# The expert down projection in three rounded passes, with its weights split in earlier stages

## The reference

```python
def grouped_moe(x, w_router, router_bias, w_gate, w_up, w_down):
    ...                                  # each row picks 2 of 16 experts, with weights comb
    for e in range(N_EXPERTS):
        h = jax.nn.silu(xt @ w_gate[e]) * (xt @ w_up[e])          # 1024 -> 256
        out = out + comb[:, e:e + 1] * (h @ w_down[e])            # 256 -> 1024

def hybrid_layer(x, ...):
    proj = x @ w_in                                               # 1024 -> 1536
    ...                                  # spatial gating and a state-space scan make the mix
    x = layer_norm(ALPHA * x + mix @ w_out, ln1_g, ln1_b)
    x = layer_norm(ALPHA * x + grouped_moe(x, ...), ln2_g, ln2_b)
```

## Time and profile before

| | us |
|---|---|
| median of 3 runs | 1359.34 |
| their range | 1359.04 to 1362.73 |
| the profiled execution: its own time | 1360.82 |
| the profiled execution: span of the instructions | 1359.2 |

### The profile page before, as it was taken

How to read it: one execution, slowest core, us unless ns; L and a number is a source line. 1 busy time by engine, 2 the same in 40 slices (tenths; PEclk the granted TensorE clock), 3 DMA queues, 4 the chain that set the end, 5 groups by cost and what they waited for, 6 DMA issues and landing times. The chain is left out here.

```text
span 1359.2 us, 22656 instructions
## 1 busy us (share of the span) xinstructions
PE 1198.9 (88%) x6653; PEld 957.0 (70%) x6654; DVE 893.2 (66%) x1975; ACT 462.5 (34%) x696; POOL 486.3 (36%) x557
## 2 busy tenths in 40 slices
PE   7999999799979768999999269999999999999910
PEld 6997999778767534888888257767767767767600
DVE  3452866468877573466667667777777777777586
ACT  4121010110012451222221225556556555556433
POOL 3008850210110033322322233545545545445267
PEclk9999899899979998999999579999999999999965
DMA  8555352564155322433332546787877777644484
GB/s 257 172 199 156 105 166 63 145 231 183 63 154 157 104 96 67 152 112 112 120 119 98 223 164 192 216 244 225 253 203 227 211 210 217 144 98 98 112 318 171
DMA packets 112875, 222.84 MB, mean 164 GB/s; under 512 B 51305, under 2 KB 68281, under 8 KB 103569
## 3 DMA queue, kind: packets, MB, share of 16 engines
q1 hardware_dynamic: 96368, 164.86, 36.3%
q0 software_dynamic: 15408, 55.12, 17.5%
q10 hardware_dynamic: 1040, 2.10, 0.4%
HBM read 144.34 MB, written 77.58 MB: 163 GB/s over the span
## 5 line engine op out<-in xcount | busy, mean ns | idle before, releaser
L2057 DVE TENSOR_TENSOR wgu<-w_raw,wgu (+1 forms) x192 | 226.0, 1219 | 52.5 <-ACT wgu L2144 52.5
L2244 PE MATMUL p_gu<-wgu,xg_high 128*128 x768 | 254.5, 413 | 4.5 <-DVE xg_low L2050 4.5
L2144 ACT CAST wgu<-w_raw (+1 forms) x192 | 187.1, 1050 | 19.4 <-SPq L1865 16.7
L2244 PEld LDWEIGHTS p_gu<-wgu,xg_high 128*128 128x128 f32 x768 | 145.2, 191 | 59.1 <-issue 31.3
L2267 PE MATMUL p_d<-wd,ht 128*128 x384 | 174.9, 598 | 1.8 <-DVE ht L2071 1.0
L2244 PE MATMUL p_gu<-wgu,xg_low 128*128 x384 | 152.0, 396 | 0.0
L2267 PEld LDWEIGHTS p_d<-wd,ht 128*128 128x128 f32 x384 | 69.0, 189 | 71.5 <-issue 71.2
L1730 PE MATMUL p_out<-w_out_high,mixt_high 128*128 128x512 f32 (+1 forms) x272 | 108.6, 399 | 10.5 <-POOL mixt_low L1507 10.5
L1730 PE MATMUL p_out<-w_out_high,mixt_low 128*128 128x512 f32 (+1 forms) x272 | 106.9, 393 | 0.0
L1730 PE MATMUL p_out<-w_out_low,mixt_high 128*128 128x512 f32 (+1 forms) x272 | 106.8, 393 | 0.0
L1936 POOL TENSOR_TENSOR spare_e<-nothing 128x1 f32<-128x1 f32 x48 | 9.3, 194 | 232.2 <-DVE yo L2077 232.2
(11 more groups left out here) (434 smaller groups left out, 2689.0 us busy)
## 6 DMA issues: line engine op xcount, KB each, us to landing
w_raw<-in_w_gate SPq DMA_DIRECT2D x16, 1024.0 KB, 4.8
w_raw<-in_w_up SPq DMA_DIRECT2D x16, 1024.0 KB, 7.7
wd<-in_w_down SPq DMA_DIRECT2D x16, 1024.0 KB, 4.7
acc_rows<-ax SPq DMA_DIRECT2D x18, 512.0 KB, 5.7
xin<-in_x_prompt SPq DMA_DIRECT2D x16, 512.0 KB, 6.3
sq<-sq_mats SPq DMA_DIRECT2D x16, 512.0 KB
z<-in_x_prompt SPq DMA_DIRECT2D x16, 512.0 KB, 4.2
x_rows<-x SPq DMA_DIRECT2D x16, 512.0 KB, 4.9
```

The costliest lines, as they stand in the source:

```text
L2057: low = tt(wgu[:, slot, 1, at], raw[:, slot, at], wgu[:, slot, 0, at].bitcast(F32), ALU.subtract)
L2144: nc.scalar.copy(wgu[:, slot, 0, at], raw[:, slot, at]).then_inc(hi_set, 1)
L2244: mm = t.matmul(pg[b][:, :, :], x[:, b, k, :], w[h][:, k], start=(k == 0 and x is xh and h == 0), stop=(k == KD - 1 and x is xl))
```

## The change

`down` is made in three rounded passes, twelve matmuls a tile. Both operands need two parts:

- `ht` becomes `ht_high` and `ht_low`. ACT makes the high part from PSUM (`hidden_high`), after three of its four weight quarters and ahead of the fourth and of `sl`. DVE's `tail` is now the subtraction, and waits for it.
- `w_down` is split before stage E, in 64 units of 128 x 512 (a quarter of an expert), and both parts go to HBM (`wd_dram`). Stage E loads 2 MB an expert where it loaded 1 MB. A unit is one load of 256 KB, a copy on ACT, a subtraction and two stores of 256 KB. 32 units are made in stage A, 8 in B (with POOL's subtraction), 24 in D, in places that are free at the time: six slots in A (two in `xin`, so that x rows have two buffers in place of four; four in parts of `ya` that are not yet written, where a row of 2 KB lies in four pieces of 512 bytes), three in B, and in D two parts of `ya` and `yb` a tile that `out` is done with (pieces of 512 bytes again). A table computed at the head of stage A gives one to two units for each step from n = 4 to 22; 21 of the 32 units are in pieces of 512 bytes.
- `ln2_g` and `ln2_b` are loaded after the last turning in place of at the head of stage E. SP's loop in D, and ACT's in B, are unrolled.

```diff
+            def units_at(n):
+                return [(j, s, sum(u[1] == s for u in UNITS[:j])) for j, (m, s) in enumerate(UNITS) if m == n]
...
+                def units(n):                                # stage A, SP
+                    for j, s, m in units_at(n - 2):
+                        sp.wait_ge(wd_low, j + 1)
+                        for h in range(2):
+                            sp.dma_start(wd_dram[h][j // 4, ...], wd_part(s, 1 - h, True).bitcast(F32)).then_inc(wd_st[s], 16)
+                    for j, s, m in units_at(n):
+                        if m:
+                            sp.wait_ge(wd_st[s], m * 32)
+                        elif s[0] == "x":
+                            sp.wait_ge(turned[int(s[1])], 1)
+                        sp.dma_start(wd_part(s, 0, False), wd_src[j // 4, :, j % 4]...).then_inc(wd_ld[s], 16)
...
                 def u_tile(i, f):                            # stage A, ACT
                     act.wait_ge(u_prod, i * FT + f + 1)
                     nc.scalar.activation(ya[:, f, i * XH:(i + 1) * XH], pu[f % 2][:, 0:XH],
                                          ACT.Gelu_apprx_tanh).then_inc(u_out, 1)
+                    for j, s, m in units_at(i * FT + f - 1):
+                        act.wait_ge(wd_ld[s], m * 16 + 16)
+                        nc.scalar.copy(wd_part(s, 1, True), wd_part(s, 0, False)).then_inc(wd_high, 1)
...
                     v.tensor_copy(ust[...], pxs[...]).then_inc(xs_out, 1)        # xs_tile, stage A, DVE
+                    for j, s, m in units_at(i * FT + f - 1):
+                        dve.wait_ge(wd_high, j + 1)
+                        v.tensor_tensor(wd_part(s, 0, True), wd_part(s, 0, False), wd_part(s, 1, True).bitcast(F32),
+                                        ALU.subtract).then_inc(wd_low, 1)
...
+                def units_in(i, b):                          # stage D, SP
+                    p = i * 2 + b
+                    sp.wait_ge(mix_low, p * 2 + 2)
+                    if p >= 5:
+                        sp.wait_ge(wd_st[b], (p - 3) // 2 * 64)
+                    for at, (e, q) in zip(areas(p), quarters(i, b)):
+                        sp.dma_start(ya[:, :, at], wd_src[bass.ds(e, 1), :, q]...).then_inc(wd_ld[b], 16)
+                def units_out(i, b):
+                    p = i * 2 + b
+                    sp.wait_ge(wd_low, p * 2 - 4)
+                    for at, (e, q) in zip(areas(p), quarters(i, b)):
+                        for h in range(2):
+                            sp.dma_start(wd_dram[h][...], (yb_r, ya_r)[h][:, :, at].bitcast(F32)).then_inc(wd_st[b], 16)
...
+                for i in range(2, CH // 2 - 1):
                     for b in range(2):
                         rows_in(i * 2 + b, b)
                         stores(i * 2 + b, b)
+                        units_out(i - 1 + b, 1 - b)
+                        units_in(i, b)
...
+                def units(i, b):                             # stage D, ACT
+                    act.wait_ge(wd_ld[b], i * 32 - 32 * (1 - b))
+                    for at in areas(i * 2 + b):
+                        nc.scalar.copy(yb_r[:, :, at], ya[:, :, at]).then_inc(wd_high, 1)
...
                         high(i * 2 + 2 + b, b)
                         tile(i * 2 + b, b, i)
                         score(i * 2 + b - 1)
+                        units(i, b)
...
+                def units(i, b):                             # stage D, DVE, after turn
+                    p = i * 2 + b
+                    dve.wait_ge(wd_high, p * 2 - 4)
+                    for at in areas(p):
+                        v.tensor_tensor(ya_r[:, :, at], ya[:, :, at], yb_r[:, :, at].bitcast(F32), ALU.subtract).then_inc(wd_low, 1)
...
                 def tail(i, b, first):                       # stage E, DVE
-                    dve.wait_ge(h_turned, i + 1)
-                    v.tensor_copy(ht[:, b], pt_h[:, :, :]).then_inc(ht_set, 1)
+                    dve.wait_ge(ht_high, i + 1)
+                    tt(ht[1][:, b], pt_h[:, :, :], ht[0][:, b].bitcast(F32), ALU.subtract).then_inc(ht_set, 1)
...
+                def hidden_high(i, b, first):                # stage E, ACT
+                    act.wait_ge(h_turned, i + 1)
+                    if not first:
+                        act.wait_ge(d_prod, i)
+                    nc.scalar.copy(ht[0][:, b], pt_h[:, :, :]).then_inc(ht_high, 1)
...
+                            for x, h in PARTS:               # stage E, PE, down
+                                mm = t.matmul(pd[m][:, :], ht[x][:, b, k, :], w[h][:, k, m * SUP:(m + 1) * SUP],
+                                              start=(k == 0 and x + h == 0), stop=(k == 1 and x == 1))
```

More of the change, by code:

```diff
@@ L266, in _ @@
                             sp.dma_start(sq_dram[pair, :, 0, :], s_mat[:, pair % 2, :]).then_inc(s_stored[pair % 2], 16)
+                        units(n)
+                        if i and f % 2 and 2 * i + 4 + f // 2 < CH:
+                            rows_in(2 * i + 4 + f // 2)
+                for s in SLOTS:
+                    sp.wait_ge(wd_st[s], sum(u[1] == s for u in UNITS) * 32)
                 sp.wait_ge(kz, 1)
@@ L396, in _ @@
                 act.wait_ge(w_v_in, 16)
+                for s in ("x2", "x3"):
+                    act.wait_ge(wd_st[s], sum(u[1] == s for u in UNITS) * 32)
                 for k in range(KD):
@@ L821, in _ @@
                 sp.wait_ge(vs_stored, 16)
+                for s in range(3):
+                    sp.wait_ge(wd_st[s], (3, 3, 2)[s] * 32)
                 sp.wait_ge(toep_in, L * 16)
@@ L1595, in _ @@
                 score(0, NS)
-                with act.Fori(1, CH // 2 - 1) as i:
+                for b in range(2):
+                    high(4 + b, b)
+                    tile(2 + b, b, 1)
+                    score(1 + b)
+                units(1, 1)
+                with act.Fori(2, CH // 2 - 1) as i:
                     for b in range(2):
@@ L1806, in hybrid_step @@
             hh = sb("hh", [P, 2, FF], where=pt)
-            ht = sb("ht", [P, 2, 2, P], where=pt)
+            ht = [sb(f"ht_{n}", [P, 2, 2, P], F32R, where=pt) for n in ("high", "low")]
+            assert pt.at <= base + 32 * KB
             pt = Place(nc, base + 35 * KB)
@@ L1874, in _ @@
                     down(e)
-                for dst, name in ((g2_row, "ln2_g"), (b2_row, "ln2_b")):
-                    sp.dma_start(dst[:], bass.AP(tensor=a[name].tensor, offset=0, ap=[[0, P], [1, D]])).then_inc(row2_in, 16)
                 for e in range(2):
@@ L1895, in _ @@
                 sp.wait_ge(prep_done, NT)
+                sp.wait_ge(x_turned, NT)
+                for dst, name in ((g2_row, "ln2_g"), (b2_row, "ln2_b")):
+                    sp.dma_start(dst[:], bass.AP(tensor=a[name].tensor, offset=0, ap=[[0, P], [1, D]])).then_inc(row2_in, 16)
                 sp.wait_ge(te_set, 3)
@@ L2139, in turn_b, with high @@
                         nc.scalar.copy(xh[:, b, h * 4:h * 4 + 4, :], pt_x[h]).then_inc(xt_hi, 1)
-                def high(slot):
-                    for c in range(4):
+                def high(slot, cs=range(4)):
+                    for c in cs:
                         at = slice(c * QG, (c + 1) * QG)
@@ L2164, in step @@
                         prep(i, not begun and b == 0, slot, ready)
+                    if begun or b:
+                        hidden_high(i - 1, 1 - b, not begun or begun == 1 and b == 0)
+                    if not last:
+                        high(slot, range(3, 4))
                     act.wait_ge(gu_prod, i + 1)
```

150 lines of the change are left out of this document (120 added, 30 removed).

## The result

The changed kernel took 1467.94 us (median of 4 runs, 1467.1 to 1468.96), the kernel before 1359.19 beside it: a ratio of 1.079 with a 95% interval of 1.078 to 1.081. The forecast of 1411 had the sign right and less than half of the size, and the range (to 1450) did not hold the time.

The account below looks back on a forecast made before the run. It took PE to bound the kernel, no stage having idle PE to hide delays. E -24, D +45, A +30, the rest +1 gave +52 on the profiled 1360.8, 1412.8, so a median of 1411, range 1365 to 1450.

Parts of the forecast that it names:

- Stage E: Expert stage: shorter `down` saves 0.5 us a tile, period 9.55, 47 periods -24 us; bounds -34 to -12.
- the 1.5 us behind it for slack: Expert tile: `xg_low` ends 1.5 us before the next `gate_up` wants it; the longer operand paths spend this.
- The late low part: Expert tile: ACT's copy then DVE's subtraction make `down` start about 0.15 us late.
- The pass: `down` in E: a rounded pass costs 0.228 us, so 12 take 2.74 for 3.46, 0.72 less.
- Rival 1: Stage E: DMA engines can't be filled past about 0.9, 10.2 us a tile, gain gone, total 1435; chance 0.16.
- the sign that I had named for it: Stage E: tiles 10 us or more apart would show the DMA-bound rival.
- Stage D: Stage D: transfers in SP's one queue form a lap of 18.4 us against 13.61 a tile, +45 us.
- the slack: Stage D: x1 is at first 4.8 us early, subtracted once from 11 laps x 4.8, about 48.
- My upper bound of +60: Stage D: with z's latency a lap of 19.5 us, +60; a lower PE clock stands inside it.
- Stage B: Stage B: eight units, with two x buffers fewer in A, cost 0 to +1 us behind PE work.
- Stage A: Stage A: units cost +11 to step 15, 16 from step 16, 3 for last stores: +30 us; bounds +10 to +45.
- The rival on the other side: Stages A and D: splitting hidden, deciding point a D lap under about 14 us, total 1336 to 1343; chance 0.10.

Follow-up runs that it names:

- x6: Changed kernel with D's loads one lap early, A's unit loads ahead of its stores, `gate_up` waiting for the fourth weight quarter only before its second half: 1382.83 us.
- x11: Changed kernel with D's loads early, ACT's fourth quarter back in place, only 21 units in A, none in B, E loading unsplit weights: 1368.94 us, E loop 481.1.
- x3: Changed kernel with `down`'s eight high-part matmuls first, the four low-part ones last behind the subtraction: 1462.96 us, E loop 484.3.
- x10: As x7, but A's units split one step later, one unit in steps divisible by four, none loaded in step 12: 1343.3 us, 0.989 of the kernel before.
- x7: Changed kernel with x3, x4 and x6's edits, 1 KB rows in A, B's subtraction on DVE, ACT's fourth quarter back in place: 1356.22 us, 0.997 of the kernel before.
- x4: Changed kernel with stage D's unit loads issued one lap ahead of ACT's copies: 1411.85 us, D 249.1.
- x5: As x4, plus 1 KB rows in A, B's POOL subtraction after `v_norm`, high-part matmuls first and split weight wait in E: 1378.05 us, E loop 463.0.

## Why the prediction was wrong

**Stage E is the step that failed.** The prediction wrote "I take 0.5 less a tile, a period of 9.55; 47 periods make -24". The traces gave 9.84 for a plain tile (from `down` to `down`, 1151.63 - 1141.79) and 10.97 for the next (1162.60 - 1151.63), which has a new expert's `gate_up` in it, as 15 of the 46 have; in the mean 10.28 against 10.16 before. Two costs were wrong, by size, and one was nearly right:

- *The fourth quarter's subtraction*, priced nowhere. I followed ACT's copy to `xg_low`, took the 1.5 us behind it for slack and stopped there. The earlier trace rows end with `xg_low`, but DVE's last instruction of a tile is that subtraction, in the kernel before too, where it left 0.39 us and not 1.5. A new expert's first product waits for it: 16 times, 0.82 us in the tile shown. The split wait (x6) brings 16 us, ACT's order alone (x11) 10.
- *The late low part*. I had 0.15; it is 0.17 to 0.24, and `down`'s first weights are then not loaded behind `p_xt`, 0.1 more. x3 removes both.
- *The pass*: 0.23 for 0.228. `down` in x3 takes 2.84 where I had 2.74, so PE gives back 0.62 of the 0.72.

Without the first two, E gains more than was hoped: 486.4 to 456.5 in x10, 30 us. Rival 1 gave almost the measured period (10.2) by a mechanism that isn't there: x3, x6 and x7 got faster at higher DMA shares (0.91, 0.91 and 0.93 from 1000 to 1100 us, where after has 0.90). That it came near is chance, and the sign that I had named for it, tiles 10 or more apart, doesn't tell the two apart. Its sum was off as well: I counted three tiles an expert, and the loads of gate and up weights come 21 to 31 us apart, for two or three.

**Stage D: right mechanism, mis-sized term.** The lap through SP's queue, ACT's wait for the unit loads and the x1 spacing are as described; x4 shows that it is all of the loss. From x1 to landed loads it is 702.64 - 689.42 = 13.2 where I had 11.5, and from ACT's unit copies' end to the end of x1 5.2 where I had 5.8; a lap of 19.1 to 19.5 for 18.4. The other error is the slack: I subtracted 4.8 once, for x1 being early in the middle of the stage. At its end it isn't early: before, the last turning began 0.06 us after its x1. So all that x1 is late counts: ten laps of 19.2 in place of 13.6 (55), the lap before them (2) and the last two together (3) make the 60. My upper bound of +60 met this by luck: it took laps of 19.5, longer than measured, and subtracted a slack that isn't there.

**Stage B: a wrong zero, and its cause in part open.** "0 to +1, behind PE work" left out that POOL's new subtraction runs beside DVE. I had the row for it, 2.01 against 0.41, and used it for stage A only. x11 shows that the units are all of the 9.5 (121.8 without them). But x5, with `vn` back at its old time, brings only 2.7 back, and x7, with the subtraction on DVE, 5. What the other 4 to 7 us are stays open. The Trainium skill, "GPSIMD Engine Reference", section "1. Specifications", names two kinds of DVE instruction that collide with GpSimd: those with two SBUF inputs and those in a 2-port perf mode. `vn` has one tensor input; the trace (1.50 against 0.55) fits the second kind, but no run here tells which mode it was in.

**Stage A: right.** +35.4 for +30, by load and latency together as put: ACT's 89 us of waits, a DMA share of 0.91 and 0.83. The terms of the +30 were 11 up to step 15, 16 behind it and 3 for the last stores; x11 says 13.5 and some 22 for the rest. The slower DVE subtractions beside POOL, for which I allowed up to 16, are there but small: eleven of the 32 take 0.9 to 2.1 us in place of 0.69, 5 us more in all. The Trainium skill's rule of 512 bytes as the smallest transfer at line rate ("DMA: Bandwidth & Descriptors", section "Specifications") was weighed against a price of 0.90 for small pieces and 0.78 for large ones. The packets of this stage side against the rule: 256 KB cost 1.00 us of the engines in pieces of 512 bytes, 0.90 in 1 KB (x5) and 0.87 in 2 KB (108.6 ns a packet), so my ratio was right and both prices some 10% low.

The rival on the other side (the splitting is hidden) had the deciding point right, a D lap under about 14, and x4 reaches it by a change of order, with one queue.

## What to carry to other kernels

A load that is issued behind stores and used in the same lap of a loop can set the lap by its latency (D: 60 us at a DMA share of 0.60, none once issued a lap ahead); issue it a lap ahead, and give it a place that is free by then. When an instruction moves down an engine's queue, follow the queue to its last instruction and ask who waits for that one, also where only some tiles do. With operands split in parts, make the products of the part that is ready first.

## What the runs showed that I had not expected

- A one-input elementwise instruction of DVE (128x512) took 1.50 us in place of 0.55 when POOL began a 1.29 us subtraction beside it, in all seven tiles where it did.
- A DMA share of 0.93 held for a whole window of 100 us in E with PE busy 99.96 us of it (x7), while in A a share of 0.91 went with holes.
- The two unit loads of a lap in D, in 512-byte pieces behind four stores, took SP 1.44 us to issue (the row at 695.61), 0.72 each, where `z` in whole rows takes 0.35; it did not set the lap, as x4 shows.
